# Other byte addresses for TensorE's stationary operands in a two-block layer

## What is computed

```python
h = _swiglu(_rms_norm(x, ffn1_pre_norm), ffn1_w_in, ffn1_w_out)       # 1024 -> 2 x 2816 -> 1024
x = x + 0.5 * _rms_norm(h, ffn1_post_norm)
m = _token_mixing(_rms_norm(x, mix_pre_norm), w_mix_in, ...)          # retention, neighbourhood attention
x = x + _rms_norm(m, mix_post_norm)
h = _swiglu(_rms_norm(x, ffn2_pre_norm), ffn2_w_in, ffn2_w_out)
x = x + 0.5 * _rms_norm(h, ffn2_post_norm)
h = rmsnorm(x, norm_g[0]); x = x + recurrent_mixer(h, ...)            # 1024 -> 2 x 1536 -> 1024
h = rmsnorm(x, norm_g[1]); x = x + shortconv_mixer(h, ...)            # 1024 -> 4 x 1536 -> 1024
return rmsnorm(x, final_g)
```

## The kernel before, in words

| tile | before | after |
|---|---|---|
| `xT` (normalised x) | 0 | 256 |
| `hT_hi`, `hT_lo`, first feed-forward | 0 | 64 |
| `hT_hi`, `hT_lo`, second feed-forward | 0 | 32 |
| `yT_hi`, `yT_lo`, recurrent mixer | 0 | 192 |
| `yT_hi`, `yT_lo`, short-convolution mixer | 0 | 384 |
| `yretT_hi`, `yretT_lo`, `ynaT_hi` | 0 | 0 |
| `ynaT_lo` (at the end of the memory) | 800 | 800 |

## Time and profile before

### The profile page before, as it was taken

The page is one execution under the profiler, slowest core; times in us unless marked ns, Lnnn a source line. Parts: engine busy times, 40 slices in busy tenths (PEclk is TensorE's granted clock), DMA queues, the critical chain, the costliest instruction groups (busy, mean ns, idle before and its releaser), DMA issues.

```text
span 887.0 us, 11473 instructions
## 1 busy us (share of the span) xinstructions
PE 879.6 (99%) x4628; PEld 752.3 (85%) x4628; DVE 625.0 (70%) x808; ACT 489.4 (55%) x661; POOL 64.4 (7%) x89
## 2 busy tenths in 40 slices
PE   9999999999999999999999999999999999999997
PEld 7888888888888888888888888888999888888886
DVE  6887776467767656577577777446979857888872
ACT  6865564445444556446565555435887644555551
POOL 2000000003021110000000000000390000000000
PEclk9999999999999999999999999999999999999999
DMA  9955555455753444455655555546534456555521
GB/s 352 368 188 191 191 189 199 147 190 179 282 198 127 180 168 173 184 190 190 237 190 190 191 190 190 189 182 251 184 106 181 151 187 254 190 190 191 190 95 48
DMA packets 26948, 169.89 MB, mean 192 GB/s; under 512 B 3616, under 2 KB 3664, under 8 KB 7952
## 3 DMA queue, kind: packets, MB, share of 16 engines
q1 hardware_dynamic: 24368, 161.23, 50.3%
q0 software_dynamic: 2240, 7.66, 2.5%
q10 hardware_dynamic: 288, 0.27, 0.1%
HBM read 167.05 MB, written 1.05 MB: 190 GB/s over the span
## 4 chain that ended last, share of the span: by engine, by line
PE 97%; DVE 1%; ACT 1%; issue 0%; ACTq 0%
PE acc L1839 15%; PE acc L1642 15%; PE acc L1640 15%; PE acc L1641 15%; PE acc L2101 8%; PE acc L1841 7%; PE acc L2103 4%; PE acc L1655 2%; PE acc L1883 2%; PE acc L2053 2%; PE acc L2054 2%; PE acc L2052 2%; PE aux L2037 1%; PE aux L1764 1%; PE acc L1885 1%; PE aux L1641 1%
## 5 line engine op out<-in xcount | busy, mean ns | idle before, releaser
L996 DVE TENSOR_TENSOR w_lo<-raw,w_hi 128x2048 fp32r<-128x2048 f32 x147 | 336.8, 2300 | 89.9 <-ACT w_hi L522 89.5
L522 ACT ACTIVATE w_hi<-raw 128x2048 fp32r<-128x2048 f32 x145 | 275.7, 1911 | 62.6 <-DMA raw<-weights 62.4
L1839 PE MATMUL acc<-xT,w_hi 128*128 128x512 f32 x576 | 200.4, 394 | 0.0
L1841 PE MATMUL acc<-xT,w_lo 128*128 128x256 f32 x576 | 159.7, 277 | 0.0
L1839 PEld LDWEIGHTS acc<-xT,w_hi 128*128 128x128 f32 x576 | 108.0, 188 | 25.0
L1640 PE MATMUL acc<-w_hi,xT 128*128 128x512 f32 x312 | 124.0, 398 | 0.0
L1642 PE MATMUL acc<-w_hi,xT 128*128 128x512 f32 x312 | 121.8, 390 | 0.0
L1641 PE MATMUL acc<-w_lo,xT 128*128 128x512 f32 x312 | 121.5, 390 | 0.0
L2101 PE MATMUL acc<-xT,w_hi 128*128 128x512 f32 x320 | 111.3, 394 | 0.0
L1841 PEld LDWEIGHTS acc<-xT,w_lo 128*128 128x128 f32 x576 | 108.2, 188 | 0.0
L2103 PE MATMUL acc<-xT,w_lo 128*128 128x256 f32 x320 | 88.7, 277 | 0.0
(11 more groups left out here) (263 smaller groups left out, 1290.4 us busy)
## 6 DMA issues: line engine op xcount, KB each, us to landing
raw<-weights SPq DMA_DIRECT2D x147, 1024.0 KB, 4.8
gain_pre<-gains POOLq DMA_DIRECT2D x5, 512.0 KB, 5.0
raw<-weights SPq DMA_DIRECT2D x4, 512.0 KB, 7.5
gain_post<-gains POOLq DMA_DIRECT2D x3, 512.0 KB, 5.6
gate_w<-gate_w_in POOLq DMA_DIRECT2D x1, 1536.0 KB, 8.5
x_turned<-x_turned_in SPq DMA_DIRECT2D x4, 256.0 KB, 4.9
x<-x_in SPq DMA_DIRECT2D x2, 512.0 KB, 11.6
bias_raw<-bias_in POOLq DMA_DIRECT2D x16, 64.0 KB, 3.2
```

Of the source, the lines that this page charges most:

```text
L522: a.activation(w_hi[:, g % RING], raw[:, g % RING], ACT.Copy).then_inc(hi_done, 1)
L996: v.tensor_tensor(w_lo[:, slot], raw[:, slot], w_hi[:, slot].bitcast(F32), ALU.subtract)\
L1839: m.matmul(dst, w_hi[:, slot, w], xT[:, k].rearrange("p a q -> p (a q)"), start=k == 0, stop=False)
L1841: i = m.matmul(dst[:, 0:S], w_lo[:, slot, w], xT[:, k, 0], start=False, stop=k == KD - 1)
```

## The change

Eleven tiles get other addresses. `xT` moves 256 bytes on, and with it all that `sb` hands out after it (`x`, the gains, the identity and the small tiles); `area` itself stays, since it is rounded up. The hidden tiles exist twice under two names, 64 bytes on for the first feed-forward and 32 for the second. The gated outputs exist twice as well, 192 bytes on in the recurrent mixer and 384 in the short-convolution mixer. What would overlap moves out of the way: the feed-forward's staging tiles by 512 bytes, half of the recurrent mixer's gated staging (`yg_4`) by 192, and the last norm's `x_scaled` and `squares`. No instruction is added, taken away or moved on any engine, no wait changes, and nothing changes in size.

```diff
+        cursor[0] += 256
         xT = sb("xT", [P, KD, 2, S], F32R)
...
-        hT_hi = at("hT_hi", [P, FF // P, S], F32R, area)
-        hT_lo = at("hT_lo", [P, FF // P, S], F32R, area + 22528)
-        silu_g = at("silu_g", [P, T, 256], F32, area + 45056)
-        prod = at("prod", [P, 2, T, 256], F32, area + 47104)
-        gate_c = at("gate_c", [P, 2, S], F32, area + 51200)
-        prod_c = at("prod_c", [P, 2, S], F32, area + 53248)
+        hidden_hi_of = {st: at(f"hT_hi_{st}", [P, FF // P, S], F32R, area + shift) for st, shift in (("f1", 64), ("f2", 32))}
+        hidden_lo_of = {st: at(f"hT_lo_{st}", [P, FF // P, S], F32R, area + 22528 + shift) for st, shift in (("f1", 64), ("f2", 32))}
+        silu_g = at("silu_g", [P, T, 256], F32, area + 45568)
+        prod = at("prod", [P, 2, T, 256], F32, area + 47616)
+        gate_c = at("gate_c", [P, 2, S], F32, area + 51712)
+        prod_c = at("prod_c", [P, 2, S], F32, area + 53760)
...
-        yg_4 = at("yg_4", [P, 2, 512], F32, area + 63488)
+        yg_4 = at("yg_4", [P, 2, 512], F32, area + 63488 + 192)
...
-        yT_hi = at("yT_hi", [P, CH, S], F32R, area + 51200)
-        yT_lo = at("yT_lo", [P, CH, S], F32R, area + 12288)
-
-        x_scaled = at("x_scaled", [P, 2, DM // 2], F32, area + 24576)
-        squares = at("squares", [P, 2, DM // 2], F32, area + 28672)
+        yT_hi_a = at("yT_hi_a", [P, CH, S], F32R, area + 51200 + 192)
+        yT_lo_a = at("yT_lo_a", [P, CH, S], F32R, area + 12288 + 192)
+        yT_hi_b = at("yT_hi_b", [P, CH, S], F32R, area + 51200 + 384)
+        yT_lo_b = at("yT_lo_b", [P, CH, S], F32R, area + 12288 + 384)
+
+        x_scaled = at("x_scaled", [P, 2, DM // 2], F32, area + 24576 + 512)
+        squares = at("squares", [P, 2, DM // 2], F32, area + 36864)
...
-                a.activation(yT_hi[:, 2 * n:2 * n + 2, :], yg[n].rearrange("p (c q) -> p c q", c=2), ACT.Copy)\
+                a.activation(yT_hi_a[:, 2 * n:2 * n + 2, :], yg[n].rearrange("p (c q) -> p c q", c=2), ACT.Copy)\
...
+                hT_hi, hT_lo = hidden_hi_of[which], hidden_lo_of[which]
...
-                out_stage(f"{which}_out", hT_hi, hT_lo, FF // P, wait_chunk, lambda: None, n + 1, 4,
+                out_stage(f"{which}_out", hidden_hi_of[which], hidden_lo_of[which], FF // P, wait_chunk, lambda: None, n + 1, 4,
...
-            out_stage("a_out", yT_hi, yT_lo, CH, lambda n: pe.wait_ge(y_low, n + 1), lambda: None, 4,
+            out_stage("a_out", yT_hi_a, yT_lo_a, CH, lambda n: pe.wait_ge(y_low, n + 1), lambda: None, 4,
...
-            out_stage("b_out", yT_hi, yT_lo, CH, lambda n: pe.wait_ge(bank_free, f0 + 2 * n + 2),
+            out_stage("b_out", yT_hi_b, yT_lo_b, CH, lambda n: pe.wait_ge(bank_free, f0 + 2 * n + 2),
```

More of the change, by code:

```diff
@@ L650, in hidden_hi @@
                 def hidden_hi(j, par):
+                    hT_hi = hidden_hi_of[which]
                     act.wait_ge(bank_full, f0 + 1 + j)
@@ L676, in chunk_round @@
                     act.wait_ge(prod_ready, c_before + n + 1)
-                    a.activation(hT_hi[:, STRAIGHT + n, :], prod_c[:, n % 2], ACT.Copy).then_inc(chunk_hi, 1)
+                    a.activation(hidden_hi_of[which][:, STRAIGHT + n, :], prod_c[:, n % 2], ACT.Copy).then_inc(chunk_hi, 1)
                 if g0 == 0:
@@ L926, in b_hi @@
                 act.wait_ge(b_y_ready, 1 + j)
-                dst = yT_hi[:, j, :] if isinstance(j, int) else yT_hi[:, bass.ds(j, 1), :].rearrange("p a q -> p (a q)")
+                dst = yT_hi_b[:, j, :] if isinstance(j, int) else yT_hi_b[:, bass.ds(j, 1), :].rearrange("p a q -> p (a q)")
                 a.activation(dst, b_y[:, par], ACT.Copy).then_inc(bank_hi, 1)
@@ L1449, in gated_lo @@
                 dve.wait_ge(bank_hi, FIRST_SPLIT["gate"] + n + 1)
-                v.tensor_tensor(yT_lo[:, 2 * n:2 * n + 2].rearrange("p c q -> p (c q)"), yg[n],
-                                yT_hi[:, 2 * n:2 * n + 2].rearrange("p c q -> p (c q)").bitcast(F32), ALU.subtract)\
+                v.tensor_tensor(yT_lo_a[:, 2 * n:2 * n + 2].rearrange("p c q -> p (c q)"), yg[n],
+                                yT_hi_a[:, 2 * n:2 * n + 2].rearrange("p c q -> p (c q)").bitcast(F32), ALU.subtract)\
                     .then_inc(y_low, 1)
@@ L1534, in b_lo @@
                 one = (slice(j, j + 1) if isinstance(j, int) else bass.ds(j, 1))
-                v.tensor_tensor(yT_lo[:, one, :].rearrange("p a q -> p (a q)"), b_y[:, par],
-                                yT_hi[:, one, :].rearrange("p a q -> p (a q)").bitcast(F32), ALU.subtract)\
+                v.tensor_tensor(yT_lo_b[:, one, :].rearrange("p a q -> p (a q)"), b_y[:, par],
+                                yT_hi_b[:, one, :].rearrange("p a q -> p (a q)").bitcast(F32), ALU.subtract)\
                     .then_inc(bank_free, 1)
```

## The result

The changed kernel takes 893.74 us (893.29 to 893.8) against 889.51 us of the kernel before in the same series. The ratio is 1.0047 with a 95% interval of 1.0036 to 1.0059: slower, by 4.2 us or 0.5%. The profiled execution has a span of 892.0 us (887.0 before).

What follows compares the result with a forecast made beforehand. TensorE's unbroken stream of matmuls was taken to bound the kernel. The second feed-forward's 1.7 us, all else 0, gave a span of 888.7 us; with 3.0 us around it, 891.7 us, range 880 to 909 for 8 in 10.

Steps and rivals of the forecast that it cites:

- C: Stages on normalised x: 256 bytes breaks the rhythm as 32 does, 21.6 us over 3,240 matmuls, time 913.4 us; chance 0.20.
- D: Toll is collision of moving stream and weight load, avoidable by another distance; on normalised x, 870 or 885.5 us; chance 0.18.
- TensorE's pitch alone sets the time: Whole kernel: one long stream of matmuls, its time their number times the distance between starts; TensorE 99% busy.
- The second feed-forward at 32: Second feed-forward's output stage: 88 triples at 0.020 us each cost 1.76 us, taken as 1.7; bounds 0 and 3.5 us.
- Normalised x at 256: Stages on normalised x, 3,240 matmuls: moving it 256 bytes on taken to cost 0.
- All of these are multiples of 64 bytes ... I take 0 for them.: Normalised x, first feed-forward's tiles and gated outputs, moved 256, 64, 192 and 384 bytes: cost 0, as nearer 0 and 512.
- The side moves at nothing: Moves of x, gains, identity, staging tiles and last norm's tiles cost nothing, covered by TensorE's chain of 97%.
- A: The forecast itself: multiples of 64 are neutral and 32 loses; 891.7 us, own range 890.0 to 893.5; chance 0.52.
- B: All stages: addresses don't matter, slow `ynaT` triples are the aftermath of a stop; time 890.0 us; chance 0.10.

## Why the prediction was right, and where it was not

The sign came out as forecast, and the time lies in the range of 880 to 909 (891.7 predicted, 893.74 measured). The size did not: the change cost 4.2 us where the sum has 1.7, and the time is just above the forecast's own range of 890.0 to 893.5. One term of the sum was put at nothing. That the time still lies in the wide range is luck in part, since its width was made for C and D, and neither happened in this kernel.

- **TensorE's pitch alone sets the time.** Right. The four output stages account for 4.4 us, close to the 4.2 timed, and the one stop above goes with weights that came later. (The 3.0 us between span and median are not all around the program: in the changed kernel the time is 1.8 us over the span of the same execution, 893.8 against 892.0. The sum doesn't suffer, since it amounts to the median plus 1.7.)
- **The second feed-forward at 32.** Right: 1.76 us forecast from the earlier trace rows, 1.69 measured. Neither bound came true: with all three loads off alike the stream found no better rhythm, and no matmul paid the dearest pitch throughout.
- **Normalised x at 256.** Right at 0. The bounds of 25 us up and 44 us down, for all that moved by a multiple of 64, were wide because no row showed such a distance.
- **"All of these are multiples of 64 bytes ... I take 0 for them."** This is the step that failed. 64 cost 1.68 us, 384 (which is 128 modulo 256) 0.78 and 192 0.28: 2.7 us that the sum lacked. The rows had only 0 and 512 on one side and 32 on the other. I put the border at 64, and by the experiments it is at 256. The one row that showed another distance than 0 or 512 had 20 ns a triple. On these 184 triples that is 3.7 us, nearer to the 2.7 measured than 0. (For 256 it would have been wrong: that price on normalised x was rival C.)
- **The side moves at nothing.** Right: with all tiles at multiples of 256, and the same side moves, the time was that of before (ratio 0.9995).

Of the rivals, **A** (multiples of 64 neutral) is right in its sign and false in its rule. **B** (addresses don't matter) is false: the first feed-forward goes from 680 to 700 with 64 bytes and back with 256. The Trainium skill (SBUF — State Buffer, Who interferes with whom) gives TensorE two independent read ports, by which no distance could have moved these stages. The 680 and 700 ns of this stream don't agree with that. What mechanism is behind the distance no run shows. **C** (256 breaks the rhythm) is false for 256, but its mechanism, a stream kept out of step, is what 64, 128 and 192 do to triples. **D** (another distance lets the two streams pass) did not happen in the changed kernel, and no triple stage settled under 680 in any run. For the chunk pairs it is half true. They went to 340 where w_hi stood 64 bytes from x (and once, in the mixer, where it stood at 192), and 340 for 512 and 256 columns is 0.2267 us per 512, exactly the triples' pace. The prediction had read the pairs of the earlier trace rows as being at the same toll as the triples, by adding 0.2267 and 0.120; but half of 0.2267 is 0.1133, so the second matmul of a pair had 0.0067 us to give all along. What is left down to the 0.215 us of the earlier trace rows no distance touched, and it stays open.

## What to carry to other kernels

Where TensorE is one unbroken stream of such triples, start from stationary and moving operands at one address modulo 256, and look at the distance between starts stage by stage, since a misplaced tile cost 1 to 3% of its stage here without showing as a wait. Compare that distance per column between kinds of matmul: a kind that is dearer per column than another may have something to gain, as the pairs had, and may want another distance than its neighbour. Read more than one execution before a step of 0.2% is put down to an address. A bound drawn from three points (0 and 512 good, 32 bad) says nothing of what lies between, so each untried value needs a price and a range of its own.

## What was not expected of the hardware

- The distances count modulo 256: 256 and 512 give 680 ns a triple like 0, while 64, as round as it looks, gives 700, and 192 gives 687.
- One misplaced load slows the whole stream. The paces met most often stand some 6.7 ns apart, 680, 687, 693 and 700 for triples and 340, 347 and 353 for pairs; others occur too, such as 691, 697 and 703, or 344 and 349.
- Pairs at distance 0 settle at 346.7 or at 353.1 with the same program, 1.7 us a stage; at w_hi 64 from x they stood at 340 in all stages in each of three kernels.
- Moving w_hi against w_lo counts beyond the distances during the loads: the high tile at 0 from w_hi and the low one at 0 from w_lo, with the two weights 192 apart, make 693, where 680 is to be had with both at one distance. What it acts by is not shown.
